# Two transformer stacks on one core: FFN loops written out, modulation weights moved into the FFNs, first loads reordered

## What is computed

```python
mod = c_act @ w_mod[l] + b_mod[l]                 # block 1: 6 groups of 1024 columns
m = jax.nn.silu(cvec) @ w_mod + b_mod             # block 2: 9 groups, for c and for c_ctx
h = modulate(rms_norm(x, ffn_norm_g[l]), sh2, sc2)
x = x + g2[:, None, :] * channel_mixer(h, w_up[l], ffn_dw_w[l], ffn_dw_b[l], w_down[l])
...
x = x + 0.5 * gate * swiglu(modulated_norm(x, g, shift, scale), w_gu, w_down)
```

## Time and profile before

| | us |
|---|---|
| runs | 3225.13, 3227.2, 3228.1 |
| median of the runs | 3227.2 |
| span of the profiled execution | 3225.6 |
| PE busy | 2880.2 (89%) |
| DVE busy | 1531.0 (47%) |
| ACT busy | 1142.0 (35%) |
| mean transfer rate | 139 GB/s |

### The profile page before, as it was taken

How to read it: one execution, slowest core, us unless ns; L and a number is a source line. 1 busy time by engine, 2 the same in 40 slices (tenths; PEclk the granted TensorE clock), 3 DMA queues, 4 the chain that set the end, 5 groups by cost and what they waited for, 6 DMA issues and landing times.

```text
span 3225.6 us, 40736 instructions
## 1 busy us (share of the span) xinstructions
PE 2880.2 (89%) x15788; PEld 2340.7 (73%) x15788; DVE 1531.0 (47%) x2262; ACT 1142.0 (35%) x1686; POOL 0.2 (0%) x4
## 2 busy tenths in 40 slices
PE   6887899998878988979999989799997999976998
PEld 3665688797655877967878755587886878764898
DVE  3669635653779356643323403333334333356454
ACT  2444425643435255533223312221223312233453
POOL 0000000000000000000000000000000000000000
PEclk9998899998988999999999999899998999988999
DMA  7551247755431457635234263122222322220453
GB/s 267 188 201 53 82 154 253 268 170 202 172 148 53 161 193 278 209 105 182 98 134 140 78 237 114 65 93 92 95 92 68 98 92 91 92 79 1 143 182 118
DMA packets 122282, 446.87 MB, mean 139 GB/s; under 512 B 13473, under 2 KB 14625, under 8 KB 121761
## 3 DMA queue, kind: packets, MB, share of 16 engines
q1 hardware_dynamic: 122144, 444.97, 39.8%
HBM read 443.87 MB, written 1.05 MB: 138 GB/s over the span
## 4 chain that ended last, share of the span: by engine, by line
PE 73%; DVE 15%; DMA 6%; ACT 3%; issue 2%; SPq 1%; ACTq 0%; DVEq 0%
PE ps L545 20%; PE ps L546 19%; PE ps L547 19%; PE ps L549 15%; DMA ring<-stream 6%; DVE area L1489 2%; DVE area L1674 2%; DVE rests L1408 2%; DVE area L1460 1%; DVE stat L1520 1%; DVE h_split L1466 1%; DVE rs L1452 1%; DVE work L1529 1%; DVE work L1516 1%; PE ps L742 1%
## 5 line engine op out<-in xcount | busy, mean ns | idle before, releaser
L545 PE MATMUL ps<-h_split,heads 128*128 128x256 f32 (+1 forms) x2992 | 1015.6, 339 | 155.6 <-DVE h_split L1466 68.8
L546 PE MATMUL ps<-h_split,heads 128*128 128x256 f32 (+1 forms) x2992 | 991.5, 331 | 0.0
L547 PE MATMUL ps<-h_split,rests 128*128 128x256 f32 (+1 forms) x2992 | 990.5, 331 | 0.0
L1408 DVE TENSOR_TENSOR rests<-ring,heads 128x1024 fp32r<-128x1024 f32 x520 | 629.1, 1224 | 644.5 <-ACT heads L1048 632.8
L545 PEld LDWEIGHTS ps<-h_split,heads 128*128 128x128 f32 x2992 | 593.1, 198 | 256.4 <-DVE h_split L1466 76.5
L1048 ACT ACTIVATE heads<-ring 128x1024 fp32r<-128x1024 f32 x520 | 538.5, 1056 | 657.2 <-PE ps L547 446.0
L546 PEld LDWEIGHTS ps<-h_split,heads 128*128 128x128 f32 x2992 | 593.9, 199 | 48.7 <-issue 3.9
L547 PEld LDWEIGHTS ps<-h_split,rests 128*128 128x128 f32 x2992 | 592.0, 198 | 46.0
L545 PE MATMUL ps<-hid_split,heads 128*128 128x256 f32 (+1 forms) x1056 | 365.0, 346 | 0.0
L547 PE MATMUL ps<-hid_split,rests 128*128 128x256 f32 (+1 forms) x1056 | 355.1, 336 | 0.0
L546 PE MATMUL ps<-hid_split,heads 128*128 128x256 f32 (+1 forms) x1056 | 354.8, 336 | 0.0
(11 more groups left out here) (156 smaller groups left out, 2159.4 us busy)
## 6 DMA issues: line engine op xcount, KB each, us to landing
ring<-stream SPq DMA_DIRECT2D x836, 512.0 KB, 3.4
consts<-constants SPq DMA_DIRECT2D x1, 2563.0 KB, 12.8
x_sb<-x_in SPq DMA_DIRECT2D x1, 1024.0 KB, 14.8
x_sb<-ctx_in SPq DMA_DIRECT2D x1, 1024.0 KB, 5.7
out<-area SPq DMA_DIRECT2D x1, 1024.0 KB, 4.8
cols<-columns SPq DMA_DIRECT2D x1, 695.5 KB, 3.7
sg<-positions_in SPq DMA_DIRECT2D x1, 128.0 KB, 3.7
```

What stands on the lines that cost most here:

```text
L545: nc.tensor.matmul(out, lhsT[0], rhs[0], start=first, stop=False)
L546: nc.tensor.matmul(out, lhsT[0], rhs[1], start=False, stop=False)
L547: ins = nc.tensor.matmul(out, lhsT[1], rhs[0], start=False, stop=last)
L1408: nc.vector.tensor_tensor(rests[:, u % RING, :], ring[:, u % RING, :], as_f32(heads[:, n % HEADS_RING, :]), ALU.subtract)\
```

## The change

The loops go: all pairs of all FFNs are written out, banks are taken in turn throughout, and waits are on constants. `guest_at` gives each FFN a table of groups, spread evenly over its 22 pairs: half a group after pair 1 and half after pair 2 of its share, the pick after pair 3. Block 1's narrow FFNs get three groups each; block 2 gets six, three, six and one, in its order of FFNs. The mixers of block 1 keep three each (after lat, uv and vb), that of block 2 none. The additions that adapt a norm's scale stand before that norm. Each input has its own semaphore, and the constants are loaded in two parts.

```diff
+FFN_MODS = {
+    "up_0": [("mod1_0", 5), ("mod1_1", 0), ("mod1_1", 1)],
+    "up_1": [("mod1_1", 5), ("mod2_0", 0), ("mod2_0", 1)],
+    "f1up_0": [("mod2_0", g) for g in (2, 3, 4, 5, 6, 7)],
+    "f2up_0": [("mod2_0", 8), ("mod2_1", 0), ("mod2_1", 1)],
+    "f1up_1": [("mod2_1", g) for g in (2, 3, 4, 5, 6, 7)],
+    "f2up_1": [("mod2_1", 8)],
+}
+def guest_at(up, j):
+    groups = FFN_MODS[up]
+    q, r = divmod(j - 1, FJ // len(groups))
+    return (groups[q], r) if j >= 1 and q < len(groups) and r < 3 else (None, None)
...
@@ sync
-            sp.dma_start(pos_i[:, :], pos_d).then_inc(inputs_landed, 16)
...
-                    if u == 1:
-                        sp.dma_start(consts[:, :], consts_d).then_inc(inputs_landed, 16)
-                        sp.dma_start(x[:, 0, :, :], x_d).then_inc(inputs_landed, 16)
+                if u == 3:
+                    sp.dma_start(x[:, 0, :, :], x_d).then_inc(x_landed, 16)
+                    sp.dma_start(consts[:, 0:tables_at], consts_d[:, 0:tables_at]).then_inc(consts_landed, 16)
+                    sp.dma_start(pos_i[:, :], pos_d).then_inc(positions_landed, 16)
+                if u == 2 * KD:
+                    sp.dma_start(consts[:, tables_at:], consts_d[:, tables_at:]).then_inc(tables_landed, 16)
@@ tensor, ffn
-                    for e in range(HEADS_RING):
-                        pe.wait_ge(vector_done, V.at(rest_step(turn[1] + e)))
-                    with T.turns(pe, (p, "up", lo), turns) as i:
...
-                    for j in range(lo + turns * PAIRS, hi):
+                    for j in range(lo, hi):
                         pair(j, [take_bank((p, kind, j)) for kind in kinds])
+                        guest, part_ = guest_at(up, j)
+                        if guest is not None and part_ < 2:
+                            mod_rows(*guest, part_)
+                        elif guest is not None:
+                            mod_cols(*guest)
@@ tensor, mixer of block 2, layer 0
-                    hook(*MIXER_MODS[2][0])
                     outs = [take_bank((p, "v", b)) for b in range(4)]
...
-                    for guest in MIXER_MODS[2][1:]:
-                        hook(*guest)
-                    hook()
-
+                    pe.wait_ge(tables_landed, 16)
@@ scalar, each_pair
                         begin(j)
-                        rest_pair(j)
+                        next_split()
+                        next_split()
                         finish(j)
```

More of the change, by code:

```diff
@@ L19 @@
[L19 removed]
+from contextlib import ExitStack
 import numpy as np
@@ L93, in weight_blocks @@
 def weight_blocks():
-    s, loops = [], []
+    s, starts = [], []
     def align(m):
@@ L227, in const_columns @@
         n += P
-    for name, size in TABLES:
+    for name, size in PICKS + TABLES:
         at[name] = (n, size)
@@ L442, in _ @@
         def _(sp):
-            sp.dma_start(cols[:, :], cols_d).then_inc(inputs_landed, 16)
-            sp.dma_start(pos_i[:, :], pos_d).then_inc(inputs_landed, 16)
-            def load(u, slot):
-                sp.dma_start(ring[:, slot, :], stream[u, :, :]).then_inc(weights_landed[slot], 16)
-            def slot_read(u):
-                if u >= RING:
[L452 to L457, removed]
+            sp.dma_start(cols[:, :], cols_d).then_inc(columns_landed, 16)
@@ L459, in _ @@
+            for u in range(units):
+                slot = u % RING
+                if u >= RING:
+                    sp.wait_ge(tensor_done, T.at(("unit", u - RING)))
+                if u == ffn_starts[1]:
                     sp.wait_ge(tensor_done, T.at(((("b1", 1), "at"), "o", 7)))
                     sp.dma_start(x[:, 1, :, :], ctx_d).then_inc(context_landed, 16)
[L461 to L477, removed]
-                    if u == 1:
-                        sp.dma_start(consts[:, :], consts_d).then_inc(inputs_landed, 16)
-                        sp.dma_start(x[:, 0, :, :], x_d).then_inc(inputs_landed, 16)
-                    u += 1
@@ L997, in _, with own, after @@
         def _(act):
-            def own(i=None):
+            def own():
                 if A.n:
-                    act.wait_ge(scalar_done, A.so_far(i))
+                    act.wait_ge(scalar_done, A.n)
             state = [0]
-            def after(S, name, turn=None):
-                if turn is None and A.loop is None:
+            def after(S, name, ahead=True):
+                if ahead:
                     for n in upcoming(state, S.unit_of(name), 5):
                         split(n)
-                    A.unit = max(A.unit, S.unit_of(name))
-                return S.at(name, turn)
+                A.unit = max(A.unit, S.unit_of(name))
+                return S.at(name)
             def prepare(p):
@@ L1430, in mod_cols @@
                                              bias.rearrange("p (r q v) -> p r q v", q=4, r=2), ALU.add),
-                     ("read", ((name, g), "cols")), i)
+                     ("read", ((name, g), "cols")))
+                if nv == 2 and g in (2, 8):
+                    step(nc.vector.tensor_scalar(out, out, 0.5, None, ALU.mult))
             pending = []
```

473 lines of the change are left out of this document (161 added, 312 removed).

## The result

The changed kernel takes 3119.6 us, the median of four runs (3116.8 to 3124.2), against 3227.7 us for the kernel before (3225.1 to 3232.3, four runs). The ratio is 0.9663, with a 95% interval of 0.965 to 0.9677.

The account below looks back on a forecast made before the run. The prediction took TensorE to bound the kernel (73% of the chain that ended last), a stage being worth its waits there. Terms sum to -77.5 us: span 3225.6 to 3148.1, plus 1.6, forecast 3150 us, range 3126 to 3179.

Parts of the forecast that it names:

- Loop entry: Between two ranges of a wide FFN: TensorE's wait for four split units goes, three entries of 3.2 us, -9.6 us.
- Mixers: Eight fewer groups in the mixers: -50.9 us in block 2, -19.9 and -9.2 us in block 1's layers 1 and 0.
- The lone group in block 1: Block 1's mixers, the group left after vb: ScalarE reads its rows 10.0 us after TensorE starts it.
- Guests in wide FFNs: Wide FFNs: 11 more groups, TensorE's own work at 5.4 us each, +59.4 us.
- that rival: Wide FFNs: closer guests wait like narrow ones, 15 groups x 3.7 us, 55 us more, 3205 us; chance 4%.
- Bank waits: Edges of wide loops: eight waits of 1.1 us in the two FFNs without guests go as banks rotate, -8.7 us.
- Second ranges and clock: Wide FFNs' second ranges: three entries, -9.6 us; low clock after two of them goes with the idle time before, -4.3 us.
- Guests in narrow FFNs: Narrow FFNs: four groups less and one more, -27.3 us; waits of 3.7 us a group mostly stay, 7 x 1.0 = -7.0 us.
- The 1.0 us that written-out code should save per group: Narrow FFNs: fewer register instructions between waits save 1.0 us for each of seven groups, -7.0 us; bounds 0 and 3.7 per group.
- First loads: Kernel start: tables moved behind unit 16 gain 0, since the bytes ahead of unit 18 stay the same; bounds -4.8 and +1.3 us.
- More gain: Narrow guests' waits vanish whole, 19 us more, and the start gives 4.8 us: 3126 us; chance 9%.
- Instruction fetches: Written-out code stalls on about 33 more fetches, 3249 us at 3 us each (2%); or loop edges cost fetches today, 3089 us (1%).

Follow-up runs that it names:

- experiment 1: Kernel before, with the last step of ScalarE and VectorE in a loop turn counting 65 instead of 1: 3201.7 us, ratio 0.9902.
- experiment 2: Changed kernel, with TensorE waiting for the norm's channel block 6 of 8 before each wide FFN's first product: 3153.4 us, ratio 0.976.
- experiment 3: Changed kernel, five groups back in block 2's mixer, layer 0; four fewer in layer 1's wide first FFN, none in the last FFN: 3146.8 us.
- experiment 11: Changed kernel, with result banks in wide FFNs starting again at the same bank after pairs 3 and 7 of a range: 3125.2 us, ratio 0.9657.
- the four parts: Changed kernel, with narrow FFN groups in four parts of two units after pairs 1 to 4, pick after pair 5: 3096.2 us, ratio 0.9581.
- Experiments 8 and 9: Changed kernel, tables loaded behind unit 24 instead of 16: 3120.5 us; then also the second start group's reading before the splits of units 17 and 18: 3115.7 us.

## Why the prediction was wrong

It forecast the right direction, but the time lies 6.4 us below its range. The terms that it named sum to -77.5 and came to -80.2. The step that failed is **Loop entry**. It read the wait of 3.02 us between ranges, explained it by the explicit waits on four split units (experiment 1 leaves it at 3.02, so that explanation stands), and then counted "three such entries". The entries behind norms were not priced. Their gaps of 16 us stood in the trace, and I took them for the norm. Two things in it should have raised the question: the narrow FFNs of block 1 stand behind a norm of half as many columns and waited only 5.25 us; and the first product needs one channel block of eight, while it started when VectorE was halfway through the seventh. The runs show what stood there: a wait for "one turn back" in a turn that has none. It held TensorE for 8.6, 9.0, 9.0 and 2.7 us, in all 29.3 of the 32.0 us by which the sum was missed, and for 0.7 more at each FFN of block 1, 1.5 of the -80.2. Experiment 1 removes it with everything else kept, and experiment 2 puts it back.

**Mixers.** Right, and for the reasons given: -82.5 against -80.0, or -81.0 without the entries of block 1's FFNs. The lone group in block 1 was priced at 10.0 us; it waits for nothing there now (4.4 us from the pick ahead of it to the products behind it), and 1.2 and 1.4 us of that are lost again in the head norms that follow.

**Guests in wide FFNs.** The price of 5.4 us was 5.1 by experiment 3. No guest waits, though they stand closer, so that rival falls.

**Bank waits.** All of them went. But the rotation of banks does this in one FFN alone (4.0 us in experiment 11); in the other two, guests stand over the edges and would have covered them.

**Second ranges and clock.** The entries are right: -9.1 against -9.6. The clock behind them is 1.00 now, but the reason given, that it was low because of the idle time before, is not shown. Experiment 1 keeps the three waits of 3.02 us, and behind the first and the third of them its clock is 0.74 and 1.00, with 19 and 25 matmuls, where it was 0.50 and 0.70 with 13 and 18:

```profile
1617.00:1622.70 5.70, 5.68 (x19) 4.64 (x20) 0.00 (x0) 0.00 (x0) 0.00 (x0) 0.74 0.00 0
...
2607.80:2613.50 5.70, 5.66 (x25) 4.71 (x26) 0.00 (x0) 0.00 (x0) 0.00 (x0) 1.00 0.00 0
```

So 2.9 of the 4.3 us went there with the waits in place (the pairs behind them took 1.3 and 1.6 us less). That the term came out is partly luck, and what lowered the clock at these two places stays open.

**Guests in narrow FFNs.** The fewer groups were priced well. The 1.0 us that written-out code should save per group is mis-sized: the row is -30.1 instead of -34.3 where fewer groups alone make -27.3, so it saved 2.8 us, 0.4 a group. Block 1's two FFNs show 10.1 and 8.2 us a group over the 129.4 us without any, on average the 9.1 of before. The reason given for the wait, that the split for pair 3 lies ten units behind, was right, as the four parts show.

**First loads.** Right, with its reason: the splits ahead of the read. Experiments 8 and 9 take away first the tables and then the splits, and the start moves by 4.6 and 7.4 us.

**Rivals.** More gain (3126 us) was right in sign, but not in its mechanism: narrow waits stayed and the start gave nothing. Instruction fetches, in either direction, had no part: 30 more transfers and no gap, and experiment 1 reaches the same entries with loops.

## What to carry to other kernels

When a loop waits for work of one turn back, look at what the first turn waits for: the value is the first turn's step less the steps of a turn, and it may name an unrelated instruction just ahead of the loop. A long idle gap ahead of a stage isn't the producer's length by itself; compare when the consumer's first operand was ready with when it started. And spread extra weights by their loading time against the products between them, since halving a burst removed a wait that removing register work did not.

## What was not expected of the hardware

Stretches that wait for transfers differ between profiled runs of kernels that do the same there: the pairs of block 1's first FFN took 157.5 to 162.6 us with halves, and the stretch from them to the next narrow FFN 484.5 to 489.2 over all kernels with the change. Stretches that wait for nothing repeat: the second range's pairs of layer 1's wide FFN took 133.1 us in each kernel that has their guests and banks alike, and the pairs of a narrow FFN with four parts 146.9 us in both layers and all three kernels. So the removal of a wait also took away most of that FFN's spread. And the written-out code fetched 2.05 MB of instructions instead of 1.56 without a stall that shows.
